# Routing of a mixture of experts: router products on rows not yet divided by the norm, in a one-core layer kernel

## The reference, cut to what matters

```python
x = x + gate1 * (mix @ p['w_out'])
h = rms_norm(x, p['norm_ffn_g']) * (1.0 + scale2) + shift2
...
logits = (h @ p['router_w']).astype(jnp.float32) + p['router_b'].astype(jnp.float32)
top_logit, top_idx = lax.top_k(logits, TOP_K)
gates = jax.nn.softmax(top_logit, axis=-1)
```

## Time and profile before

| | |
|---|---|
| time, median of 3 runs | 1275.15 us (1272.76 to 1277.76) |
| the profiled execution's own time | 1273.2 us |
| its span, first to last instruction | 1271.4 us |
| PE busy | 1176.2 us (93%) |
| DVE, ACT busy | 314.8 us (25%), 210.6 us (17%) |
| mean granted clock of TensorE | 0.983 |
| DMA, mean over the span | 362 GB/s |

### The profile page before, as it was taken

The page is one execution under the profiler, slowest core; times in us unless marked ns, Lnnn a source line. Parts: engine busy times, 40 slices in busy tenths (PEclk is TensorE's granted clock), DMA queues, the critical chain, the costliest instruction groups (busy, mean ns, idle before and its releaser), DMA issues.

```text
span 1271.4 us, 17024 instructions
## 1 busy us (share of the span) xinstructions
PE 1176.2 (93%) x7124; PEld 474.1 (37%) x7124; DVE 314.8 (25%) x644; ACT 210.6 (17%) x360; POOL 39.4 (3%) x70
## 2 busy tenths in 40 slices
PE   4979998888999999999999999999999999999995
PEld 1425577664433333333333333333333333333321
DVE  1203758644212112111211111111211111111113
ACT  1102254521111111111111111111111111111112
POOL 0200100000000000000000000000000000000000
PEclk9989999898999999999999999999999999999998
DMA  9899000159699999999999999999999999999992
GB/s 372 305 329 390 13 2 14 66 198 418 261 404 431 428 429 428 428 428 429 429 429 429 430 428 430 429 429 429 429 429 429 430 428 429 430 430 430 429 428 124
DMA packets 44397, 460.16 MB, mean 362 GB/s; under 512 B 5129, under 2 KB 7345, under 8 KB 16577
## 3 DMA queue, kind: packets, MB, share of 16 engines
q1 hardware_dynamic: 41296, 451.98, 84.6%
q0 software_dynamic: 2576, 6.41, 1.8%
q10 hardware_dynamic: 480, 1.13, 0.2%
HBM read 458.03 MB, written 1.47 MB: 361 GB/s over the span
## 4 chain that ended last, share of the span: by engine, by line
PE 59%; DMA 33%; DVE 5%; issue 1%; ACT 1%; SPq 0%; ACTq 0%; DVEq 0%
DMA ring<-in_moe_w_gu_dram 27%; PE bank L1222 22%; PE bank L1246 13%; PE bank L604 5%; PE bank L1180 3%; PE bank L1165 3%; DMA ring<-in_w_mod_dram 3%; PE bank L1202 2%; DMA ring<-in_w_in_dram 1%; PE bank L579 1%; DMA proj<-in_norm_ffn_g_dram 1%; PE bank L1173 1%; PE bank L718 1%; DVE proj L2124 1%; PE bank L592 1%
## 5 line engine op out<-in xcount | busy, mean ns | idle before, releaser
L1222 PE MATMUL bank<-ring,proj 128*64 128x512 f32 x1536 | 341.5, 595 | 17.2 <-DMA ring<-in_moe_w_gu_dram 16.1
L1222 PEld LDWEIGHTS bank<-ring,proj 128*64 128x64 f32 x1536 | 105.7, 137 | 250.5 <-issue 209.6
L1246 PE MATMUL bank<-ring,proj 128*64 128x512 f32 x768 | 175.4, 598 | 8.4 <-DVE proj L2124 8.4
L2115 DVE TENSOR_SCALAR proj<-bank 128x512 f32<-128x512 f32 x32 | 22.1, 692 | 462.0 <-PE bank L1222 462.0
L1586 ACT ACTIVATE proj<-proj 128x512 f32<-128x512 f32 x32 | 20.2, 630 | 590.0 <-DVE proj L2115 590.0
L604 PE MATMUL bank<-ring,param_sb 128*128 128x512 f32 (+2 forms) x224 | 89.6, 555 | 0.2 <-DMA ring<-in_w_in_dram 0.2
L1246 PEld LDWEIGHTS bank<-ring,proj 128*64 128x64 f32 x768 | 51.4, 136 | 98.7 <-issue 93.8
L2128 DVE COPY proj<-bank 128x512 f32<-128x512 f32 x32 | 22.1, 691 | 247.9 <-PE bank L1246 247.9
L1180 PE MATMUL bank<-proj 64*128 64x512 f32 x256 | 63.6, 615 | 0.8 <-DVE proj L2128 0.8
L1222 PE MATMUL bank<-param_sb,proj 128*64 128x512 f32 x256 | 57.9, 594 | 6.0 <-DMA param_sb<-in_moe_w_gu_dram 6.0
L1165 PE MATMUL bank<-h_nat,proj 128*64 128x512 f32 x264 | 62.3, 592 | 0.9 <-DVE proj L2097 0.9
(11 more groups left out here) (343 smaller groups left out, 919.3 us busy)
## 6 DMA issues: line engine op xcount, KB each, us to landing
ring<-in_moe_w_gu_dram SPq DMA_DIRECT2D x96, 2048.0 KB, 31.3
ring<-in_moe_w_down_dram SPq DMA_DIRECT2D x48, 2048.0 KB, 35.2
const_sb<-in_moe_w_gu_dram SPq DMA_DIRECT2D x16, 2048.0 KB, 31.3
param_sb<-in_moe_w_gu_dram SPq DMA_DIRECT2D x16, 2048.0 KB, 32.2
ring<-in_w_mod_dram SPq DMA_DIRECT2D x12, 2048.0 KB, 15.4
const_sb<-in_moe_w_down_dram SPq DMA_DIRECT2D x8, 2048.0 KB, 35.2
param_sb<-in_moe_w_down_dram SPq DMA_DIRECT2D x8, 2048.0 KB, 35.2
ring<-in_w_in_dram SPq DMA_DIRECT2D x5, 2048.0 KB, 17.3
```

Source lines behind the costliest of these rows:

```text
L1222: mm = pe.matmul(b[CAP * half:CAP * half + CAP, :], xT[:, k % 4, k // 4, :], w[:, 2048 * kc + o + 512 * half:2048 * kc + o + 512 * half + ...
L1246: mm = pe.matmul(b_down[CAP * half:CAP * half + CAP, :], aT[:, k % 4, k // 4, :], w[:, D * kc + 512 * half:D * kc + 512 * half + 512], sta ...
L2115: ts(moe["glu"], bank[4][:, :], LIMIT, None, ALU.min).then_inc(sem("glu_sb"), 1)
```

## The change

It alters the routing stage and adds its preparations to the front:

- **Front.** The norm's weight is loaded (two DMAs by POOL) beside the modulation rows, and DVE multiplies it into the scale row there, on 64 partitions by 512, before SP writes the row out. PE turns the shift rows (job `shT`, 4 transposes) and multiplies them by the router's weights (job `shW`, 8 products of 2 rows by 32). DVE adds the router's bias, and POOL writes these two rows to DRAM, waits, and loads them back onto all partitions.
- **Routing.** The 512 KB load of the norm's weight onto all partitions is gone, and so are the two multiplications at line 2025. The residual is made in halves of 512 columns, and PE turns u, as soon as a half is there. The router's products run on u for each group in its own bank; the logits are scaled by r and the prepared row is added when DVE reads them. The h that the experts need is made aside. `keep_busy(9)`, `(2)` and `(2)` become three of `(1)`. The choice is made for each group by itself, and the gates after the positions and the first `one_hot`. The barrier is gone.
- **Places.** The one-hot matrices and the turned gates move to `mod_sb`.

```diff
-    jobs += [("proj", 3, 0), ("rw_loraT", 0), ("proj", 3, 1), ("rw_loraT", 1), ("rw_wa", 0, 0), ("rw_wa", 0, 1), ("rw_g", 0)]
-    jobs += [("proj", 4, 0), ("rw_wa", 1, 0), ("rw_wa", 1, 1), ("rw_g", 1), ("proj", 4, 1)] + halves(0)
+    jobs += [("proj", 3, 0), ("rw_loraT", 0), ("proj", 3, 1), ("rw_loraT", 1), ("shT",), ("rw_wa", 0, 0), ("rw_wa", 0, 1), ("rw_g", 0)]
+    jobs += [("proj", 4, 0), ("rw_wa", 1, 0), ("rw_wa", 1, 1), ("rw_g", 1), ("shW",), ("proj", 4, 1)] + halves(0)
...
-    jobs += [("h2T", s, h) for s in range(2) for h in range(2)]
-    jobs += [("router",), ("pos",)]
+    jobs += [("h2T", 0, 0), ("h2T", 0, 1), ("h2T", 1, 0), ("router", 0), ("h2T", 1, 1), ("router", 1), ("pos",)]
...
-        def end_phase(eng, k):
-
-            eng.drain().then_inc(phase, 1)
-            eng.wait_ge(phase, 3 * (k + 1))
...
+                if g == 2:
+                    sp.wait_ge(sem("gain_rows"), 1)
...
-            sp.dma_start(ffn_g, a["norm_ffn_g"][0].unsqueeze(0).to_broadcast([P, D])).then_inc(sem("mod2_in"), 16)
...
-            sp.wait_ge(sem("x2_sq"), 2)
-            sp.wait_ge(full[jobs["router",] % ROT], jobs["router",] // ROT + 1)
+            sp.wait_ge(sem("x2_sq"), 4)
+            sp.wait_ge(full[jobs["router", 1] % ROT], jobs["router", 1] // ROT + 1)
...
+            after(pool, "modT")
+            for s in range(2):
+                pool.dma_start(mod_sb[s:s + 33:32, 0, :], a["norm_ffn_g"][0].rearrange("(q n) -> q n", q=2)) \
+                    .then_inc(sem("ffn_in"), 16)
...
+            pool.wait_ge(sem("router_row"), 1)
+            pool.dma_start(bias_dram, router_row).then_inc(sem("router_row_out"), 16)
+            pool.wait_ge(sem("router_row_out"), 16)
+            pool.dma_start(router_add, bias_dram.unsqueeze(0).to_broadcast([P, 2, NE])).then_inc(sem("router_add_in"), 16)
...
+            def router_rows():
+
+                after(pe, "shT")
+                b = open_bank(pe, "shW")
+                shT = early["modT"].rearrange("p (c q m) -> p c q m", c=4, q=4)
+                for c in range(KC):
+                    mm = pe.matmul(b[0:2, 0:NE], shT[:, c % 4, 2 + c // 4, 0:2], router_w[:, c, :], start=(c == 0), stop=(c == KC - 1))
+                filled(mm, "shW")
...
+            pe.wait_ge(sem("mod_sb"), 2)
+            transposes(("shT",), [mod_sb[:, 1, P * c:P * (c + 1)] for c in range(4)])
...
+            router_rows()
...
-            for s in range(2):
-                if s:
-                    keep_busy(9)
-                pe.wait_ge(sem("h2"), s + 1)
-                for part in range(2):
-                    transposes(("h2T", s, part), [h[:, s, P * c:P * c + P] for c in range(4 * part, 4 * part + 4)])
-            b = open_bank(pe, "router")
-            for s in range(2):
-                for part in range(2):
-                    after(pe, "h2T", s, part)
+            def turn_u(s, part):
+
+                pe.wait_ge(sem("u2"), 2 * s + part + 1)
+                transposes(("h2T", s, part), [scale2[:, s, P * c:P * c + P] for c in range(4 * part, 4 * part + 4)])
+
+            def router(s):
+                b = open_bank(pe, "router", s)
                 for c in range(KC):
-                    mm = pe.matmul(b[:, NE * s:NE * s + NE], hT[:, s, c, :], router_w[:, c, :],
-                                   start=(c == 0), stop=(c == KC - 1))
-            filled(mm, "router")
-
-            keep_busy(2)
+                    if c % 4 == 0:
+                        after(pe, "h2T", s, c // 4)
+                    mm = pe.matmul(b[:, 0:NE], hT[:, s, c, :], router_w[:, c, :], start=(c == 0), stop=(c == KC - 1))
+                filled(mm, "router", s)
+
+            turn_u(0, 0)
+            turn_u(0, 1)
+            turn_u(1, 0)
+            router(0)
+            keep_busy(1)
+            turn_u(1, 1)
+            router(1)
+            keep_busy(1)
             pe.wait_ge(sem("chosen"), 1)
             b = open_bank(pe, "pos")
             before = C("earlier")
             pe.matmul(b[:, 0:NE], before, selm[:, 0, :], start=True, stop=True)
-            pe.matmul(b[:, NE:2 * NE], ones, selm[:, 0, :], start=True, stop=False)
-            pe.matmul(b[:, NE:2 * NE], before, selm[:, 1, :], start=False, stop=True)
-            pe.matmul(b[:, 2 * NE:3 * NE], ones, selm[:, 0, :], start=True, stop=False)
-            filled(pe.matmul(b[:, 2 * NE:3 * NE], ones, selm[:, 1, :], start=False, stop=True), "pos")
-            keep_busy(2)
-            end_phase(pe, PH_ROUTE)
...
+            pe.wait_ge(sem("h2"), 2)
             gather()
+            pe.wait_ge(sem("xe_sb"), 1)
+            turn(b_misc, moe["xe"]).then_inc(sem("xeT_full"), 1)
+            pe.wait_ge(sem("gate_ready"), 1)
             for s in range(2):
                 mm = pe.transpose(b_down[0:NE, P * s:P * s + P], gate[:, s, :], ident)
             mm.then_inc(sem("gateT_full"), 1)
-            pe.wait_ge(sem("xe_sb"), 1)
-            turn(b_misc, moe["xe"]).then_inc(sem("xeT_full"), 1)
+            for name in (("h2T", 0, 0), ("h2T", 0, 1), ("h2T", 1, 0), ("router", 0), ("h2T", 1, 1), ("router", 1), ("pos",)):
+                after(pe, *name)
...
+            def squares(s, part):
+
+                o = slice(512 * part, 512 * part + 512)
+                act.wait_ge(sem("x2"), 2 * s + part + 1)
+                A(gate1[:, s, o], x[:, s, o], ACT.Square, accum_out=sel_e["b"][:, 2 * s + part:2 * s + part + 1]).then_inc(sem("x2_sq"), 1)
+
+            def root(s):
+                act.wait_ge(sem("var2"), s + 1)
+                A(sel_e["b"][:, 4 + s:5 + s], sel_e["b"][:, 4 + s:5 + s], ACT.Sqrt, scale=float(D)).then_inc(sem("rstd2"), 1)
+
+            def turned_u(s, part):
+                b = take(act, "h2T", s, part)
+                done(A(hT[:, s, 4 * part:4 * part + 4, :], b[:, :].rearrange("p (c t) -> p c t", c=4), ACT.Copy), "h2T", s, part)
+
+            squares(0, 0)
+            squares(0, 1)
+            root(0)
+            squares(1, 0)
+            turned_u(0, 0)
+            turned_u(0, 1)
+            squares(1, 1)
+            turned_u(1, 0)
+            root(1)
+            turned_u(1, 1)
+            act.wait_ge(sem("shifted"), 2)
             A(sel_e["e4"], sel_e["e4"], ACT.Exp).then_inc(sem("exp4"), 1)
-            end_phase(act, PH_ROUTE)
...
+            b = take(dve, "shW")
+            tt(router_row, b[0:2, 0:NE], Pm("router_b")[0:2], ALU.add).then_inc(sem("router_row"), 1)
+            dve.wait_ge(sem("router_row"), 1)
+            done(dve.nop(), "shW")
...
+            dve.wait_ge(sem("ffn_in"), 32)
+            dve.wait_ge(sem("mod_sb"), 3)
+            stt(out=mod_sb[0:64, 2, :], in0=mod_sb[0:64, 2, :], scalar=1.0, in1=mod_sb[0:64, 0, :],
+                op0=ALU.add, op1=ALU.mult).then_inc(sem("gain_rows"), 1)
...
+            def residual(s, part):
+
+                o, k = slice(512 * part, 512 * part + 512), 2 * s + part + 1
+                b = take(dve, "out", s, part)
+                step(tt(gate1[:, s, o], gate1[:, s, o], b[:, :], ALU.mult))
+                done(dve.nop(), "out", s, part)
+                tt(x[:, s, o], x[:, s, o], gate1[:, s, o], ALU.add).then_inc(sem("x2"), 1)
+                dve.wait_ge(sem("x2"), k)
+                if k == 1:
+                    dve.wait_ge(sem("mod2_in"), 16 * 4)
+                tt(sc[:, s, o], x[:, s, o], sc[:, s, o], ALU.mult).then_inc(sem("u2"), 1)
+
+            def variance(s):
+                dve.wait_ge(sem("x2_sq"), 2 * s + 2)
+                step(ts(var[:, s:s + 1], ss[:, 2 * s:2 * s + 1], ss[:, 2 * s + 1:2 * s + 2], D * EPS, ALU.add, ALU.add))
+                dve.reciprocal(var[:, s:s + 1], var[:, s:s + 1]).then_inc(sem("var2"), 1)
+
+            def rows2(s):
+                dve.wait_ge(sem("rstd2"), s + 1)
+                stt(out=h[:, s, :], in0=sc[:, s, :], scalar=var[:, s:s + 1], in1=h[:, s, :], op0=ALU.mult, op1=ALU.add) \
+                    .then_inc(sem("h2"), 1)
+
+            def choose(s):
+
+                b = take(dve, "router", s)
+                dve.wait_ge(sem("rstd2"), s + 1)
+                step(stt(out=lg[:, s, :], in0=b[:, 0:NE], scalar=var[:, s:s + 1], in1=router_add[:, s, :], op0=ALU.mult, op1=ALU.add))
+                done(dve.nop(), "router", s)
+                step(dve.max(m8[:, s, :], lg[:, s, :]))
+                step(dve.max_index(idx8[:, s, :], m8[:, s, :], lg[:, s, :]))
+                step(dve.tensor_copy(idxf[:, s, :], idx8[:, s, 0:4]))
+                step(tt(one8[:, s], bc(C("iota_e"), [P, TOPK, NE], 1), bc(idxf[:, s], [P, TOPK, NE], 2), ALU.is_equal))
+                step(dve.tensor_reduce(selm[:, s, :], one8[:, s].rearrange("p k e -> p e k"), AX.X, ALU.add))
+                dve.nop().then_inc(sem("chosen"), 1)
+                tt(e4[:, s, :], m8[:, s, 0:4], m8[:, s, 0:1].to_broadcast([P, 4]), ALU.subtract).then_inc(sem("shifted"), 1)
+
+            residual(0, 0)
+            residual(0, 1)
+            variance(0)
+            residual(1, 0)
+            rows2(0)
```

(16 more changed lines are left out.)

109 lines of the change are left out of this document (33 added, 76 removed).

## The result

The changed kernel takes 1259.34 us (1257.54 to 1260.45), the kernel before 1274.22 (1272.76 to 1277.76). The ratio is 0.987 (0.986 to 0.989): 14.9 us off by the medians, where 10 were forecast. The profiled execution has a span of 1257.8 us, an own time of 1259.41 and a mean granted clock of 0.986. By spans 13.6 us are gone.

What follows compares the result with a forecast made beforehand. The expert weight stream bounds the end, its early hole set by routing. Gain 12 us at full clock, 8.4 at low clock, 10 taken: 1273.2 - 10 = 1263.2, or 1265.2 by the median; forecast 1264, range 1259 to 1270.

Steps and rivals of the forecast that it cites:

- what bounds the kernel: Expert weight stream: full from 680 to 1240 us; ending routing earlier pays one for one while its early hole (13.6 us) lasts.
- T + 6.8: Routing, full clock: second group's router products end 6.8 us after T, the last output product's end (308.6).
- T + 10.6: Routing, full clock: the gather starts 10.6 us after the last output product's end, 3.8 after the router's last product.
- T + 15.8: Routing, full clock: first expert's weights multiplied 15.8 us after the last output product's end, at 324.4, 14.2 earlier.
- the thirteenth piece at 348.9: SP's queue, full clock: homes come free 14.2 us earlier, so the thirteenth expert weight load goes out at 348.9.
- ready for it: Weight stream without holes: could take the thirteenth load at 350.0, 13.1 us earlier (13.6 + 1.2 - 1.7).
- The clock: Routing: 1.2 GHz from about 4 us after the last output product, costing 5.8 us; first weights 330.2, gain 8.4.
- Splitting the difference to 10: Whole kernel: 10 us gain taken, between 12 at the full clock and 8.4 with the clock low until the gather's end.
- the hole closes altogether: Rival on the weight stream: clock holds, front costs 1.2 only, 13.6 us off, 1260 to 1261; chance 0.16.
- the sign of the front: Front: added PE and DVE work makes everything from 145 us on, the stream's start included, 1.7 us later (1.2 to 2.6).
- the stop taken as nothing: PE's 2.18 us instruction stop at 267.44 may move, perhaps into routing; bounds nothing to 2.2, nothing taken.
- The check at the entry into the experts' loop: Experts' loop: the skill's rule implies a stop at entry; the trace disagrees, first loop expert starting 27.6 after the previous.

Runs made afterwards that it cites:

- b_thin: Kernel before with only its fillers cut, keep_busy 9, 2 and 2 to 1, 1 and 1; slower by 0.4%.
- b_both: Kernel before with fillers cut to 1, 1 and 1 and the norm's weight folded into the scale rows in the front; executions 1268.2 to 1282.3 us.
- a_bar: Changed kernel with the barrier of PE, ACT and DVE back and the gates ahead of the positions; 4.8 us slower by medians.
- b_pad40: Kernel before with 40 empty instructions at PE's start; its measured time is not given in the text.
- b_pad24: Kernel before with 24 empty instructions at PE's start; profiled execution 1277.1 us, 4.6 more than its median.
- b_mm12: Kernel before with twelve transposes of the identity matrix at PE's start, into a bank nobody reads; 0.1% (0 to 0.2%) gained.
- b_gain: Kernel before with only the norm's weight folded into the scale rows in the front, without its 512 KB load and two products; 7.5 us faster.
- a_old: Changed kernel with the old 9, 2 and 2 fillers in place of 1, 1 and 1; 5.6 us slower by medians.
- a_h: Changed kernel with the router's products on h in place of u, prepared rows still made but unread; time that of the changed kernel.
- a_hold: Changed kernel with two more dense filler products, between the first gather and the first expert's bias; 1260.01 us.
- a_lean: Changed kernel with router products on h and without shT, shW, DVE's sum and POOL's write and read of the rows; 1258.4 us.

## Why the prediction was right and where it was wrong

**Right: what bounds the kernel.** The end hangs on the thirteenth piece one for one, with 906.9 to 908.5 us behind it in all fourteen profiles.

**Right: the sum of routing at the full clock.** "T + 6.8" for the second group's products was 6.3, "T + 10.6" for the gather 10.0, "T + 15.8" for the first weights 15.76, though there with some luck: from the gather to first weights it took 5.8 and not 5.1. The thirteenth piece came at 349.96, 13.1 earlier. That the step before the clock's had "the thirteenth piece at 348.9", and the stream "ready for it" at 350.0, is luck: T was 3 us earlier than it said and the first expert 4.1 longer, and the stream was not full then (182 GB/s from 348 to 352).

**Wrong: the step "The clock".** It put the fall to 1.2 GHz at T + 4, in the thin products of routing, charged 5.8 us ahead of the first weights (330.2), and left the 24.5 us behind them as they were. The clock was 1.00 until 320 us, well behind the start of the gather (315.59), and the first weights came at T + 15.76. The step read the earlier trace rows as if both falls there would recur, though the one at 310 came with a wait of PE for DVE, as did those of b_thin (3.88, 3.76 us), b_both (4.80) and a_bar (2.69), and the change takes that wait away. b_pad40, b_pad24 and b_mm12 have the wait too (3.83 to 4.25) and the fall with it. The other kind, thin work alone, is seen in b_gain, after 4.4 us of both groups' transposes and products in a row; it came in three of the five profiles with that code and full fillers (before, b_pad24, b_gain), and not in b_pad40 and b_mm12. The change breaks this work up, with a filler behind each group's products (PE's timeline has them at 308.58 and 311.72), and the clock held up to the gather's wait in all seven profiles of it and its variants. That the fillers at these places are the reason is argued, not shown. What the step left out is behind: in after the falls in the first expert made it 4.1 longer than in the profile that the forecast started from, 2.8 of it in the products. But those 24.5 us were themselves the shortest of four profiles of the same code (24.46 to 28.92). So 5.8 were charged where none came, and the term behind was taken from one fortunate execution. Splitting the difference to 10 left the case "the hole closes altogether" at 0.16; by its number (13.6 off) it is about what happened, though not as it said, since a hole was left, and by another sum: 1.3 and 16.0 less, 4.1 more, and 0.5 less behind. The 14.9 of the medians lie just beyond the 14 at which the range ended, although 1259.34 itself is above its 1259: the base of 1273.2 was a little below the median.

**Not settled: the sign of the front.** The stream was to start 1.7 later; in this pair of profiles it started 1.3 earlier (276.13). The terms: PE's added work 1.1 us (0.56 for shW against 1.0 taken), less a load's wait of 0.48 that was gone; DVE's product moved the heads' wait from 1.04 to 1.83, 0.8 against 0.7. That makes 1.4, and 145.63 against 145.19 is only 0.4. The heads' products then took 3.18 at a low clock, 1.2 more. Against this, L780 to the stream's start took 12.0 and not 14.7: 1.4 by the moved stop, the rest by a low clock behind it (0.66 on the mean of 272 to 276 before) that this execution did not have. But a pair is too little here. The heads' products start at 144.7 to 146.2 in the four profiles with the old front (before, b_thin, b_pad40, b_pad24) and at 145.6 to 148.0 in the five with the new one (after, a_old, a_bar, a_h, a_hold), the stream at 276.4 to 277.8 and at 276.1 to 279.1. By the means the new front is 1.1 late at the heads and 0.4 at the stream, with the 1.4 of the moved stop between: near the prediction's sum for the front, with a gain that it did not have.

**Wrong: the stop taken as nothing.** The text said that a change of the order puts it elsewhere, and bounded it by nothing and a loss. In the mixers it was a gain: about 1.4 us in a_lean's 13.4 against 12.0, and 0.9 to 1.5 in b_mm12's 12.3 against the 13.2 to 13.8 of the others of before at the full clock. The check at the entry into the experts' loop was also the weaker one, as the program runs into the loop in order. The loop first jumps back ahead of the ninth expert, and PE shows no stop there either: its weights start at 561.37, 27.6 after the eighth's.

**What the parts are worth.** Against the changed kernel the old fillers cost 7.2 us of routing, the barrier with the old order of the gates 5.2 (2.6 of wait, 2.6 of low clock), products on h 0.9. From the other side the folded weight alone gives 6.4, and fewer fillers alone nothing but a loss. They are not a sum: with the folded weight alone the fillers could not go (b_both), with the halves and the new order besides they could. The halves were not tested by themselves.

**Open.** Why the clock falls in the first expert's products. Of the nine profiles without hold_clock whose clock was full at the gather, after, a_lean, b_pad40 and b_mm12 lost it there, and before, b_gain, b_pad24, a_h and a_old did not. As the same code stands on both sides, it differs from execution to execution, and a single profile of a variant says little about it. With hold_clock two of two held, which is too few to call these fillers the cause. Why 2.8 us saved there do not show in the median is open too: the profiled execution is one, T differs between executions by more than that (305.2 to 308.6 among the changed kernels), and the other executions of the changed kernel may not have lost the clock. No version here is measurably faster than the changed kernel; a_lean does the same with less.

## What to carry to other kernels

Before pricing a filler or a clock, find the wait beside it: fillers in front of a wait for another engine hold the clock, and the same fillers cost their full length once the wait is gone, so the two edits must be made and judged together. Find the one issue behind which the time is constant, and write every edit as a shift of it. Test the clever part by itself: here an algebraic identity gave the change its name and 0.9 us of routing, while a load taken off the path, the fillers, and the barrier with the order of the choice gave several us each. And take the base of a sum from more than one execution: a term read in one profile was 2.8 to 4.5 us longer in three others of the same code.

## What the runs showed of the hardware beyond that

Twelve small products at the start of a program, some 260 us ahead, move a stop of PE in the second mixer and shorten it from about 2 us to about 1, in straight-line code. During the eight stops at the old place the w_out load runs at 406 to 412 GB/s; at the new one it is about to end: in the half microsecond behind each of the six stops the DMA engines move 25 to 66 GB/s. Empty instructions (24, 40) do not move it. The Trainium skill, Runtime: NRT & Kernel Launch, section Instruction fetch mechanics, says that crossing from one block of instructions to the next is mostly hidden. If these stops are such crossings, which no view shows, they are not hidden here: all fourteen profiles have one of 0.81 to 2.18 us ahead of the stream. Why empty instructions don't count for its place is open.

The granted clock of one and the same code differs between executions: in four profiles of it the first expert's 64 rows took 13.95, 15.64, 13.95 and 15.65 us, and the four rows of filler behind the router's products 3.44, 1.96, 3.50 and 1.96.
